# q, k, v products of the first block by seven block products in place of eight, one more spare weight tile, and a row turn at another place

## What is computed

```python
def first_block(x, ...):                     # x: 256 x 1024
    for i in range(2):
        u = rmsnorm(h, norm_mix[i])
        if i == 0: h = h + dsw_mixer(u, a_w_qkv, ...)    # qkv = u @ w, w: 1024 x 4608
        else:      h = h + moba_mixer(u, b_w_qkv, ...)   # qkv = u @ w, w: 1024 x 3072
        h = h + sq_relu_mlp(rmsnorm(h, norm_ffn[i]), ffn_w1[i], ffn_w2[i])
# of each expert e, for its tokens xb (up to 64 in a block here):
        hid = jax.nn.silu(xb @ w_gate[e]) * (xb @ w_up[e])     # 1024 x 512, twice
        y   = hid @ w_down[e]                                  # 512 x 1024
```

## Time and profile before

| what | us |
|---|---|
| median of 3 runs | 2286.58 |
| lowest and highest of them | 2282.37, 2296.83 |
| the profiled execution, its own time | 2287.61 |
| its span in the trace (first to last instruction) | 2285.8 |
| PE busy (share of the span) | 2075.1 (91%) |
| DVE, ACT, POOL busy | 747.2 (33%), 381.7 (17%), 230.4 (10%) |
| bytes moved by DMA, mean rate | 631.60 MB, 276 GB/s |

### The profile page before, as it was taken

The page is one execution under the profiler, slowest core; times in us unless marked ns, Lnnn a source line. Parts: engine busy times, 40 slices in busy tenths (PEclk is TensorE's granted clock), DMA queues, the critical chain, the costliest instruction groups (busy, mean ns, idle before and its releaser), DMA issues.

```text
span 2285.8 us, 22290 instructions
## 1 busy us (share of the span) xinstructions
PE 2075.1 (91%) x8720; PEld 1086.5 (48%) x8720; DVE 747.2 (33%) x1569; ACT 381.7 (17%) x820; POOL 230.4 (10%) x270
## 2 busy tenths in 40 slices
PE   8999999999999999899988889889488898999886
PEld 3456666444666667345433334334254443334332
DVE  1125774114687225864311011101443311111102
ACT  2232000114100121651100000000332100000001
POOL 2000000000010000430121111111000111111110
PEclk9999999999999999999899899999799899999988
DMA  9663888442688612112799999999743799999996
GB/s 314 239 162 92 303 304 301 165 147 92 227 300 303 223 50 78 70 41 107 305 394 408 401 409 386 405 410 416 277 175 146 274 417 421 421 409 369 415 420 252
DMA packets 129467, 631.60 MB, mean 276 GB/s; under 512 B 14900, under 2 KB 17108, under 8 KB 103024
## 3 DMA queue, kind: packets, MB, share of 16 engines
q1 hardware_dynamic: 108352, 579.29, 64.6%
q0 software_dynamic: 18048, 33.30, 5.2%
q10 hardware_dynamic: 2992, 18.02, 2.1%
HBM read 625.46 MB, written 26.57 MB: 285 GB/s over the span
## 4 chain that ended last, share of the span: by engine, by line
PE 68%; DMA 22%; DVE 6%; ACT 3%; issue 2%; SPq 0%; ACTq 0%; DVEq 0%; POOLq 0%
DMA ring<-ex_up 21%; PE PS L1220 15%; PE PS L542 12%; PE PS L915 10%; PE PS L904 9%; PE PS L842 4%; PE PS L1238 4%; PE PS L2158 2%; PE PS L1210 1%; PE PS L880 1%; PE PS L832 1%; DVE arena L2483 1%; PE PS L700 1%; PE PS L1229 1%; DVE arena L805 1%
## 5 line engine op out<-in xcount | busy, mean ns | idle before, releaser
L1220 PE MATMUL PS<-ring,arena 128*64 128x512 f32 x992 | 486.9, 648 | 89.8 <-DMA ring<-ex_up 87.4
L1223 PE MATMUL PS<-ring,arena 128*64 128x512 f32 x1008 | 494.7, 649 | 0.0
L1220 PEld LDWEIGHTS PS<-ring,arena 128*64 128x64 f32 x992 | 142.1, 149 | 367.8 <-issue 353.5
L542 PE MATMUL PS<-ring,arena 128*128 128x512 f32 (+1 forms) x736 | 297.6, 560 | 6.9 <-DMA ring<-a_w_qkv 1.9
L1549 DVE COPY arena<-PS 128x512 f32<-128x512 f32 x64 | 44.3, 692 | 631.7 <-PE PS L1210 631.7
L1238 PE MATMUL PS<-ring,arena 128*64 128x512 f32 x1008 | 230.2, 599 | 1.5 <-DVE arena L1545 1.5
L915 PE MATMUL PS<-ring,arena 128*128 128x512 f32 x512 | 222.6, 593 | 0.0
L542 PEld LDWEIGHTS PS<-ring,arena 128*128 128x128 f32 x736 | 138.1, 192 | 145.1 <-issue 138.0
L904 PE MATMUL PS<-arena,ring 128*128 128x256 f32 x896 | 196.9, 381 | 0.0
L904 PEld LDWEIGHTS PS<-arena,ring 128*128 128x128 f32 x896 | 169.6, 190 | 32.3 <-issue 10.1
L915 PEld LDWEIGHTS PS<-ring,arena 128*128 128x128 f32 x512 | 97.2, 190 | 114.9 <-issue 114.2
(11 more groups left out here) (276 smaller groups left out, 1835.1 us busy)
## 6 DMA issues: line engine op xcount, KB each, us to landing
ring<-ex_up SPq DMA_DIRECT2D x63, 2048.0 KB, 22.5
ring<-ex_down SPq DMA_DIRECT2D x63, 2048.0 KB, 23.3
ring<-ex_gate SPq DMA_DIRECT2D x62, 2048.0 KB, 17.5
ring<-ffn_w SPq DMA_DIRECT2D x32, 2048.0 KB, 12.7
ring<-mod_w SPq DMA_DIRECT2D x24, 2048.0 KB, 8.2
ring<-a_w_qkv SPq DMA_DIRECT2D x8, 2048.0 KB, 25.1
ring<-b_w_qkv SPq DMA_DIRECT2D x6, 2048.0 KB, 9.4
ring<-w_in_ab SPq DMA_DIRECT2D x3, 2048.0 KB, 8.9
```

What stands on the lines that cost most here:

```text
L542: mm = pe.matmul(PS[:, u % 4, 0:w.width], q.src[:, k, w.t * P:(w.t + 1) * P], w8(w.tile, w.width)[:, k, :], start=(k == 0), stop=(k == KD ...
L1220: g = pe.matmul(PS[0:CAP, u, :], xT[:, k, :], gate[k], start=(k == 0), stop=(k == KD - 1))
L1223: h = pe.matmul(PS[CAP:P, u, :], xT[:, k, :], up[k], start=(k == 0), stop=(k == KD - 1))
```

## The change

1. **q, k, v.** Layer a keeps two single units (its tile 0) and takes its other eight tiles in four *quads*; layer b takes its six tiles in three quads. A quad is 2 column tiles by 2 token tiles, seen as a 2 x 2 block product also over the two halves of the 1024 rows. It is formed by 7 products of 4 matmuls (`p1, n5, p7, p6, p2, p3, p4`) where four units had 8 of that size. For this DVE makes four sums of parts of x per layer (`s1..s4`, into `modacc`), and per quad sums of weight blocks (`t1, t2, t4` of 2 x 128x1024 each; in a layer's first quad `t3` too) into a third ring slot or over a part of the tile; in the other quads POOL makes `t3` as one 128x2048 sum. Seven joins per quad on DVE (128x512, PSUM or SBUF) put the four results together in SBUF, so that the head norm multiplies from SBUF; ACT copies `p1` and `n5` out of PSUM. In layer b the first quad's `t1, t2` are made among the last residual adds of the feed-forward part, and ACT turns out the fourth piece of raw x ahead of the second square.
2. **Spare tiles.** `gate_a` of the first MoE and `up_a` of the second become spare tiles as well, so `middle` loads two ring tiles and one ring tile. For this `ARENA` grows from 19352 to 22424. ACT issues three quarters of `gate_a` ahead of the first MoE and the rest at its start.
3. **Rows turned elsewhere.** `turn_mod(1)` moves into the feed-forward part of layer b (before the products of the last tile), and its `modulation` into `ctx_out`.
4. **GpSimd's DMAs.** The area for its descriptors is 4096 bytes in place of the default (`SCRATCH`), and the store of the bias rows goes out in DMAs of 8 heads each (3 and 2 in place of 1 and 1).

```diff
-ARENA = 19352
+ARENA = 22424
+SCRATCH = 4096
...
-        T_aqkv = R.tiles(9)
+        quad_tiles = lambda n: [R.tiles(3) for _ in range(n)]
+        T_aqkv = R.tiles(1)
+        Q_aqkv = quad_tiles(4)
         T_awo = R.tiles(1)
         T_ffn = [None, None]
-        T_bqkv = T_bwo = None
...
-                T_bqkv = R.tiles(6)
+                Q_bqkv = quad_tiles(3)
...
-        ring_parts = (("gate_a", "up_a", "down_b"), ("up_a", "down_b"))
+        ring_parts = (("up_a", "down_b"), ("down_b",))
...
+        def pe_quads(pe, q, behind=None):
+            raw, singles = q.raw, q.units[0:len(q.units) - 4 * len(q.quads)]
+            def turn(w):
+                if w.qk:
+                    pe_turn_heads(pe, q, w)
+            for u, w in enumerate(singles):
+                at(pe, *(raw.done if u else raw.first))
+                at(pe, q.halves)
+                for k in range(KD):
+                    if k == KD // 2 and u == 0:
+                        pe_raw_turn(pe, raw, 2)
+                        pe_raw_turn(pe, raw, 3)
+                        tile_full(pe, w.tile)
+                    mm = pe.matmul(PS[:, u, :], q.src[:, k, w.t * P:(w.t + 1) * P], w8(w.tile)[:, k, :],
+                                   start=(k == 0), stop=(k == KD - 1))
+                mm.then_inc(w.done[0], 1)
+                if behind and u == 0:
+                    behind()
+                if u == 1:
+                    turn(singles[0])
...
+            def product(bank, x, w, done, between=None):
+                for k in range(4):
+                    if between and k == 2:
+                        between()
+                    mm = pe.matmul(PS[:, bank, :], x[:, k, :], w[:, k, :], start=(k == 0), stop=(k == 3))
+                mm.then_inc(done[0], 1)
+            for g in q.quads:
+                last = q.quads[g.i - 1] if g.i else None
+                tile_full(pe, g.a)
+                if last:
+                    at(pe, last.c11.done)
+                    product(0, q.x["11"], g.a1, g.p1)
+                    turn(last.c22)
+                elif singles:
+                    at(pe, *singles[0].free)
+                    product(0, q.x["11"], g.a1, g.p1)
+                    at(pe, *singles[1].free)
+                else:
+                    at(pe, *raw.first)
+                    pe_raw_turn(pe, raw, 2)
+                    product(0, q.x["11"], g.a1, g.p1, between=lambda: pe_raw_turn(pe, raw, 3))
+                    at(pe, *raw.done)
+                if last:
+                    at(pe, last.c12.done)
+                at(pe, q.mixed["s1"], q.mixed["t1", g.i])
+                product(1, q.s1, g.t1, g.n5)
+                if last:
+                    turn(last.c12)
+                    at(pe, last.c21.done)
+                elif singles:
+                    turn(singles[1])
+                at(pe, q.mixed["s3"], q.mixed["t3", g.i])
+                product(2, q.s3, g.t3, g.p7)
+                if last:
+                    turn(last.c21)
+                    at(pe, last.u2)
+                tile_full(pe, g.scratch)
+                at(pe, q.mixed["s2"])
+                product(3, q.s2, g.t2, g.p6)
+                at(pe, g.p1_copied, q.mixed["t4", g.i])
+                product(0, q.x["12"], g.a2, g.p2)
+                at(pe, g.n5_copied, q.mixed["s4"])
+                tile_full(pe, g.b)
+                product(1, q.s4, g.b2, g.p3)
+                at(pe, g.u3)
+                product(2, q.x["22"], g.t4, g.p4)
+                turn(g.c11)
...
+            for name in names:
+                if name in needs:
+                    at(dve, q.mixed[needs[name]])
+                out, a, b, op = terms[name]
+                dve.tensor_tensor(out, a, b, op).then_inc(q.z.mixed, 1)
...
+            out, a, b = {"t1": (g.t1, g.a1, g.b1), "t2": (g.t2, g.t1, g.b2), "t3": (g.t3, g.b1, g.b2),
+                         "t4": (g.t4, g.t2, g.a2)}[name]
...
+                dve_mix_weights(dve, q, g, "t4")
+                mix("t1", 0, 1)
+                join(three, one, PS[:, 3, :], ALU.add, [g.p1_copied, g.p6], older.c12.free if older else ())
+                join(four, three, PS[:, 2, :], ALU.add, [g.u2, g.p7], older.c21.free if older else ())
+                join(three, two, three, ALU.subtract, [g.u3, g.n5_copied])
+                join(two, two, four, ALU.subtract, [g.v2])
+                join(one, one, PS[:, 0, :], ALU.add, [g.p2])
+                dve_head_norm(dve, q, g.c11, own, lambda: mix("t2", 0))
+                join(three, three, PS[:, 1, :], ALU.add, [g.p3])
+                dve_head_norm(dve, q, g.c22, own, lambda: mix("t2", 1))
+                join(four, four, PS[:, 2, :], ALU.add, [g.p4])
+                dve_head_norm(dve, q, g.c12, own)
+                dve_head_norm(dve, q, g.c21, own)
...
+        def pool_quads(pool, q):
+            for g in q.quads[1:]:
+                at(pool, q.mixed["t1", g.i])
+                tile_full(pool, g.b)
+                flat = [x.rearrange("p k n -> p (k n)") for x in (g.b1, g.b2)]
+                pool.tensor_tensor(flat[0], flat[0], flat[1], ALU.add).then_inc(q.z.b_summed, 1)
...
+            if stored:
+                pe.wait_ge(s.mod_row, b0.mod_row + MOD_N // 2)
+                stored()
...
+        always_free = [(eighths(19352, 6), 0), (eighths(7168, 2), 6)]
         spare_pieces = (
-            dict(down_a=[(area(0, 4, D), 0)],
+            dict(gate_a=always_free,
...
+                 up_a=always_free,
...
+            def quad_loads(w, quads, first):
+                for i, (a, b, _) in enumerate(quads):
+                    load(a, columns(w, (first + 2 * i) * BANK))
+                    load(b, columns(w, (first + 2 * i + 1) * BANK))
...
-            pe_ffn(pe, f_b, tail=ctx_norm)
+            pe_ffn(pe, f_b, tail=ctx_norm, stored=lambda: turn_mod(1, 2))
             def gated_products(stream, c):
                 first = 4 * (stream == 0)
             for c in range(1, 4):
                 gated_products(0, c)
             at(pe, *glu_done)
-            turn_mod(1, 7)
-            pe.wait_ge(s_mod.copied, 2)
...
-            raw_rows(n_b1)
-            act_qkv(act, q_b)
+            act_raw_square(act, n_b1, 0)
+            act_raw_out(act, n_b1, 1)
+            act_raw_out(act, n_b1, 3)
+            act_raw_square(act, n_b1, 1)
+            act_raw_root(act, n_b1)
+            act_quads(act, q_b)
...
+            spare_load(act, moes[0], "gate_a", 0)
...
+            own = own_steps(dve)
+            at(dve, *n_a1.done)
+            dve_mix_sums(dve, q_a, "s1", "s3", "s2", "s4")
+            dve_head_norm(dve, q_a, q_a.units[0], own)
+            dve_mix_weights(dve, q_a, q_a.quads[0], "t1")
+            dve_mix_weights(dve, q_a, q_a.quads[0], "t2")
+            dve_mix_weights(dve, q_a, q_a.quads[0], "t3")
+            dve_head_norm(dve, q_a, q_a.units[1], own)
+            dve_quads(dve, q_a, own)
...
+            def mix_ahead(t, h):
+                if (t, h) == (0, 0):
+                    dve_mix_weights(dve, q_b, q_b.quads[0], "t1")
+                elif (t, h) == (0, 1):
+                    dve_mix_weights(dve, q_b, q_b.quads[0], "t2")
...
+            at(dve, *n_b1.done)
+            dve_mix_sums(dve, q_b, "s1", "s3")
+            dve_mix_weights(dve, q_b, q_b.quads[0], "t3")
+            dve_mix_sums(dve, q_b, "s2", "s4")
             dve_raw_scales(dve, n_b1)
-            dve_qkv(dve, q_b)
+            dve_quads(dve, q_b, own)
...
-                src = bass.AP(tensor=rows.tensor, offset=rows.offset + P - 1,
-                              ap=[[ARENA, dst.shape[0]], [-1, P], [1, SEQ]])
-                pool.dma_start(dst, src).then_inc(s_bd, 16)
+                for first in range(0, dst.shape[0], 8):
+                    src = bass.AP(tensor=rows.tensor, offset=rows.offset + first * ARENA + P - 1,
+                                  ap=[[ARENA, 8], [-1, P], [1, SEQ]])
+                    pool.dma_start(dst[first:first + 8], src).then_inc(s_bd, 16)
...
+    nc = bacc.Bacc("TRN2", target_bir_lowering=False, num_devices=1, dynamic_dma_scratch_size=SCRATCH)
...
```

More of the change, by code:

```diff
@@ new lines, in dve_head_norm @@
+        def dve_head_norm(dve, q, w, own, between=None):
+            if not w.qk:
+                if between:
+                    between()
+                return
+            dve.wait_ge(q.s.square, q.b.square + w.n + 1)
+            dve.tensor_reduce(stat(0, w.n), q.squares[:, w.n % 2, :].rearrange("p (h d) -> p h d", h=8), AX, ALU.add)\
+               .then_inc(q.s.sum, 1)
+            if between:
+                between()
+            dve.wait_ge(q.s.root, q.b.root + w.n + 1)
+            own(dve.reciprocal(stat(3, w.n), stat(2, w.n)))
+            own.wait()
+            if w.n >= 3:
+                dve.wait_ge(q.s.turned, q.b.turned + w.n - 2)
+            at(dve, w.done)
+            dve.tensor_tensor(q.normed[:, w.n % 3, :].rearrange("p (h d) -> p h d", h=8),
+                              w.src.rearrange("p (h d) -> p h d", h=8),
```

(17 more changed lines are left out.)

219 lines of the change are left out of this document (177 added, 42 removed).

## The result

The changed kernel takes 2315.3 us (median of 5 runs, 2310.2 to 2318.5) beside 2288.0 for the kernel before (5 runs): a ratio of 1.010, 95% interval 1.008 to 1.013. It is slower by 27 us where 25 less were forecast, and outside the range of 2255 to 2274. The profiled execution took 2315.7 with a span of 2313.9, so 28.1 us more of span.

A forecast was written before the change was run, and what follows sets the result against it. PE was taken to bound both layers' products, the weight stream both MoEs. Layer a -8.5, layer b -9.2, turned rows -2.1 and spare tiles -5.0 and 0 made -24.8 on a span of 2285.8: 2262 us, range 2255 to 2274.

The forecast's parts named there:

- the split store: GpSimd's bias rows stored in several DMAs: costed at nothing, with the landing staying at 51.8 us.
- step (3): Layer a, SBUF port shared by GpSimd and DVE: POOL's `t3` holds up a DVE join in quad 0; 1.0 us, bounds 0 and 2.4.
- The slower rival: MoE gathers and scatters: the small descriptor area makes each wait for its predecessor's landing; 180 us more, 2440; chance 0.04.
- step (1), the start: Layer a's start: PE waits at `n5` for DVE's first sums and head norms; 3.0 us, 2.7 to 3.2.
- (2), the clock: Layer a, behind the stall at the start: matmuls run slower for a while; 0.5 us, bounds 0 and 1.7.
- (4), the end: Layer a's end: a DVE join now stands ahead of the last copy on ACT; 0.7 us.
- the lock-out rival: Quads: DVE and GpSimd lock each other out in every quad; +7 to +10 us, 2271; chance 0.16.
- Layer b: Layer b's q, k, v products: 10.3 us of matmuls dropped, less small costs; -9.2 us, -9.7 to -5.
- The turned rows: Scores of block 2, layer 0: PE's wait for DVE's small copy goes; -2.1 us, -4.4 to 0.
- The spare tiles: MoE weight streams: one ring tile fewer gains 5.0 us in the first MoE (bounds -5.4 to 0), 0 in the second.
- the 0.48 for faster: Whole kernel: the chance given to a time over 1% faster, under 2263.7 us.

The follow-up runs named there:

- row_split: The changed kernel with the bias store cut by rows (four DMAs of 24 partitions x 32 rows, two of 16 x 64) in place of heads: 2274.8 us.
- pool_between: The changed kernel with only GpSimd's order in layer a changed, `t3` of quads 1 and 2 placed right behind the second and third store: 2296.4 us, one run.
- t3_dve: The changed kernel, slow store by heads kept, with DVE making all `t3` and GpSimd none: 2286.4 us, 0.9985 of the kernel before.
- best: row_split with `t3` on DVE, unit 1's head norm and `t3` ahead of `t2` at layer a's start, next quad's `t1` behind three joins: 2268.0 us; again 2273.9.

## Why the prediction was wrong

**The step that failed** is the sentence that costs the split store at nothing: "POOL has nothing else to do then, and the landing at 51.8 is set by its bytes." Neither half holds. The landing is not set by bytes: a third of the bytes took 26.3 us where all took 27.5. And what stands behind it in GpSimd's order is no longer only the loads, for which 147 us is early enough, but `t3`. The prediction even names the landing at 51.8 as the point from which `t3` starts, in its step (3), without asking whether that edit moves it. It cost 39.2 us of wait, 1.6 of slow clock, and part of the 3.4 + 2.9 at 58 us through late weights; row_split, where only this is mended, measures 40.5 us less (39 by the ratios, 0.993 and 1.010, each to the kernel before beside it).

**The slower rival** had the right mechanism at the wrong place. A small area made GpSimd wait in its issue; I looked for it at the gathers and scatters of the MoE, where the issue stayed at 960 and 1008 ns (952 and 1005 before). The words on "a DMA of the split store 1024, for which the area must be enough as well" were meant as an argument against it, and were the hint: enough for one is not enough for the next.

**Layer a, step (1), the start**: 3.0 forecast, 2.2 measured; right in place and cause, though under its own bound of 2.7. **(2), the clock**: 0.5 forecast; 0 in the changed kernel at that wait (3.70), 1.7 in row_split (5.30 for the same products), both inside the bounds. **(3), the port**: 1.0 forecast with 2.4 as the bound; in row_split 3.5 of wait and 1.7 of clock behind it, so 5.2, over the bound. I had the room of the turn right but let the DVE instruction be held for a part of the sum, where it ran 5.7 us longer, more than the whole sum of 4.5. Whether it is held depends on which instruction falls beside the sum: in row_split it came in one quad of three, in pool_between in two, as the lock-out rival has it. **(4), the end**: the wait of 1.63 in place of 0.87 is the 0.7.

**Layer b**: -9.2 forecast, -9.2 measured (+37.3 to +28.1). **The turned rows**: -2.1 forecast, -4.6 measured, just over the bound of -4.4 of that step; of the chain of 2 us that I left in place only 1.0 was waited for, and the slow scores behind the wait (2.08 for 1.13) were gained as well. **The spare tiles**: -5.0 in the first MoE forecast; 2.6 there in one pair of profiles, less than two profiles of the same MoE code differ by, and none in the medians. The backlog of 4.4 us at 1402 stands in its row, but that it turns into time is not borne out, and the slow clock ahead of the next scores, 2 to 3 us in all but one profile with the tiles, was no term of the sum.

**The rest of the sum**: row_split is the change as I had pictured it, at 2274.8 against 2262 forecast. The 13 us between are 4.6 of waits and slow products in layer a (9.1 measured, 4.5 forecast), the spare tiles' 5, 2.3 us by which layer a's attention took longer (39.8 for 37.5, at a mean clock of 0.91 for 0.95; for this I have no cause), less 2.5 for the turned rows; some 3 more lie in the kernel before, whose median beside row_split was 2291.4 where the forecast started from 2286.6. These parts are added up, not tested one by one, because it sets parts of one profile against a median, and the profiled run of row_split (2284.7) is the slowest of its seven. In that profile row_split is 14.7 us ahead at the scores of block 2, layer 0, where 19.8 were forecast, but only 2.3 at the last hidden values of the second MoE, which alone takes 7.3 us longer (460.4 for 453.1). The split of what comes behind block 2's scores stays open. In the chances, the 0.48 for faster comes to 0.46 by its own parts.

## What to carry to other kernels

A DMA that is split or moved has to be followed to whatever stands behind it in its engine's order, and to the transfers beside it, even when its own landing has tens of microseconds of room: another edit may just have put something behind it that has no such room. Split a transfer so that each part keeps all source partitions; parts by partition took as long as the whole (26.3 us each, and 27.5). And a sum on GpSimd is not free beside VectorE instructions with two SBUF inputs: one of them ran 5.7 us longer beside a sum of 4.5, which costs more than the 2.4 us that VectorE itself takes for the same sum.

## What the runs showed of the hardware

- A store of 1 KB rows from 8 partitions: 26.3 us for 1024 rows, at 40 GB/s; one of 24 partitions: 27.5 us for 3072 rows, at 114 GB/s.
- With a descriptor area of 4096 bytes, a second store of 1024 rows from 8 other partitions waited in GpSimd's issue until the first had landed (25.8 and 27.3 us); three of 768 rows from 24 partitions were issued within 2.6 us.
- Weight tiles beside a store from 8 partitions landed in 32.5 us (t3_dve), beside one from 24 in 14.9 and 18.0 (row_split, best).
- A VectorE sum of 128x1024 took 6.89 us beside a GpSimd sum of 4.52, and 1.22 alone; two joins with both inputs in SBUF took 4.51 beside such a sum and 1.42 alone, two with one input in PSUM 1.40 either way. GpSimd's sum of 128x2048 took 4.5, less than four times its 1.33 for 128x512 in the earlier trace rows.
- The same products between the MoEs ran at a granted clock of 1.00 over their first 5 us in six profiles and of 0.50 to 0.66 in seven, all seven with the additional spare tiles.
